# A hybrid retention / attention layer on one core: the opening rebuilt by channel pairs, and transposes woven into three projections

## What is computed

```
mod  = silu(c) @ w_ada + b_ada                    # 6 x 1024; one vector for latents, one for the prompt
h    = rmsnorm(x) * (1 + scale1) + shift1
proj = h @ w_in                                   # q_r,k_r | v_r | g_r | q_d | k_d | v_d | gates
branch_r = (silu(g_r) * group_norm(retention)) @ w_ret_out
branch_d = rmsnorm(diff_attention) @ w_diff_out
x  = x + gate1 * ((gate_r * branch_r + gate_d * branch_d) @ w_o)
h2 = rmsnorm(x) * (1 + scale2) + shift2
x  = x + gate2 * ((silu(h2 @ w_gate) * (h2 @ w_up)) @ w_down);  y = rmsnorm(x)
```

## Time and profile before

| | |
|---|---|
| the profiled execution's own time | 1375.61 us |
| its span (first to last instruction) | 1373.9 us |
| PE busy, PEld busy | 1307.0 us (95%), 1199.1 us (87%) |
| DVE, ACT, POOL busy | 635.4 (46%), 420.0 (31%), 179.8 (13%) |
| share of PE in the chain that ended last | 83% |
| mean granted TensorE clock | 0.986 |

### The profile page before, as it was taken

The page is one execution under the profiler, slowest core; times in us unless marked ns, Lnnn a source line. Parts: engine busy times, 40 slices in busy tenths (PEclk is TensorE's granted clock), DMA queues, the critical chain, the costliest instruction groups (busy, mean ns, idle before and its releaser), DMA issues.

```text
span 1373.9 us, 20027 instructions
## 1 busy us (share of the span) xinstructions
PE 1307.0 (95%) x7974; PEld 1199.1 (87%) x7974; DVE 635.4 (46%) x1001; ACT 420.0 (31%) x642; POOL 179.8 (13%) x189
## 2 busy tenths in 40 slices
PE   4899999999999999998999799899999999999996
PEld 1599887799999999987788798799998999889995
DVE  3734121466657634372898554452224232343245
ACT  5422233344321122213777222242221121212222
POOL 1002000310001011111899200000000000000000
PEclk9999999999999999998999999999999999999998
DMA  9534222143334443452000215111222122221211
GB/s 299 160 103 121 90 64 75 38 154 122 115 130 143 130 121 97 125 188 85 2 2 1 93 62 184 62 62 61 84 69 92 62 69 84 72 82 62 76 46 77
DMA packets 87180, 129.27 MB, mean 94 GB/s; under 512 B 3465, under 2 KB 64386, under 8 KB 86994
## 3 DMA queue, kind: packets, MB, share of 16 engines
q1 hardware_dynamic: 76800, 95.20, 21.3%
q0 software_dynamic: 9104, 32.20, 7.5%
q10 hardware_dynamic: 1218, 1.07, 0.2%
HBM read 117.43 MB, written 4.73 MB: 89 GB/s over the span
## 4 chain that ended last, share of the span: by engine, by line
PE 83%; POOL 6%; DVE 5%; ACT 2%; DMA 2%; issue 1%; DVEq 0%; SPq 0%; ACTq 0%
PE psum L382 50%; PE psum L411 26%; POOL probs L733 3%; POOL probs L739 2%; PE psum L363 1%; DVE ada_acc L1234 1%; DMA x_nat<-in_x_prompt 1%; PE psum L481 1%; PE psum L482 1%; DMA x<-in_x_prompt 1%; PE psum L835 1%; PE psum L833 0%; PE psum L834 0%; DVE hf L524 0%; ACT junk L969 0%
## 5 line engine op out<-in xcount | busy, mean ns | idle before, releaser
L347 DVE TENSOR_TENSOR w_lo<-w_raw,w_hi 128x2048 fp32r<-128x2048 f32 x78 | 178.7, 2291 | 341.5 <-ACT w_hi L342 333.5
L382 PE MATMUL psum<-h_hi,w_lo 128*128 128x320 f32 x1344 | 307.9, 310 | 4.0 <-DVE hf L524 1.4
L382 PE MATMUL psum<-h_lo,w_hi 128*128 128x320 f32 x1344 | 306.8, 309 | 0.0
L382 PE MATMUL psum<-h_hi,w_hi 128*128 128x320 f32 x1344 | 306.8, 309 | 0.0
L382 PEld LDWEIGHTS psum<-h_hi,w_lo 128*128 128x128 f32 x1344 | 225.0, 188 | 5.4 <-issue 4.4
L382 PEld LDWEIGHTS psum<-h_hi,w_hi 128*128 128x128 f32 x1344 | 225.3, 188 | 0.0
L382 PEld LDWEIGHTS psum<-h_lo,w_hi 128*128 128x128 f32 x1344 | 225.1, 188 | 0.0
L342 ACT ACTIVATE w_hi<-w_raw 128x2048 fp32r<-128x2048 f32 x77 | 146.9, 1908 | 209.8 <-PE psum L411 158.5
L411 PE MATMUL psum<-w_lo,h_hi 128*128 128x512 f32 x240 | 93.7, 390 | 0.4 <-ACT mod L1042 0.4
L411 PE MATMUL psum<-w_hi,h_hi 128*128 128x512 f32 x240 | 93.4, 389 | 0.0
L411 PE MATMUL psum<-w_hi,h_lo 128*128 128x512 f32 x240 | 93.4, 389 | 0.0
(11 more groups left out here) (234 smaller groups left out, 1836.3 us busy)
## 6 DMA issues: line engine op xcount, KB each, us to landing
w_raw<-in_w_in SPq DMA_DIRECT2D x32, 1024.0 KB, 5.7
ada_b<-in_w_ada POOLq DMA_DIRECT2D x32, 512.0 KB, 4.0
w_raw<-in_w_ffn_gate SPq DMA_DIRECT2D x11, 1024.0 KB, 5.2
w_raw<-in_w_ffn_up SPq DMA_DIRECT2D x11, 1024.0 KB, 5.2
ada_a<-in_w_ada SPq DMA_DIRECT2D x8, 1024.0 KB, 12.1
w_raw<-in_w_ffn_down SPq DMA_DIRECT2D x8, 1024.0 KB, 4.8
w_raw<-in_w_ret_out SPq DMA_DIRECT2D x4, 1024.0 KB, 4.7
swapped<-qk_d POOLq DMA_DIRECT2D x32, 128.0 KB, 2.5
```

The lines of the kernel that those rows point to most:

```text
L347: dve.tensor_tensor(w_lo[s][:, :, :], w_raw[s][:, :, :], w_hi[s][:, :, :].bitcast(F32), ALU.subtract).then_inc(w_lo_done, 1)
L382: last = pe.matmul(bank(4 * par + 2 * j + h, HALF), w[:, k, cs], x[:, k, h * HALF:(h + 1) * HALF], start=(k == 0 and n == 0), stop=(k == K ...
```

## The change

- SP loads x first, tile by tile, then the first weight tile of w_in, then the tiles of w_ada in pairs: tile n of shift1 and tile n of scale1, which hold the channels of blocks 2n and 2n + 1. The tables and POOL's rope table come later; ACT loads all small rows.
- Six of the eight tiles are now computed directly as columns: `ada_columns` has 128x128 pieces of w_ada as weights and the 2 columns of silu(c) as moving data (16 matmuls a tile). The other two go through DVE as before.
- The transposes of x come early and are copied to SBUF (`x_T`). DVE and ACT modulate pair by pair (`modulate_pair`).
- The first projection works block by block: for each k three of the four halves of units 0 and 1, between them the later `ada_columns`; the fourth half follows at the end. DVE's rotation, split and `setup` of qk_r change order.
- At yg, od and h2 `pe_T_and_dense` issues three blocks of transposes, and then one further block behind each block of products (k + 3 behind k). `dve_to_T_shifted`, `act_to_T_shifted` and DVE's loop for od are as they were.
- ret_out comes ahead of gate_d, right behind the transposes of yg.

```diff
-          ("gate_r", 4, "act", "act"), ("gate_d", 4, "act", "act"), ("ret_out", 4, "dve", "dve"),
+          ("gate_r", 4, "act", "act"), ("ret_out", 4, "dve", "dve"), ("gate_d", 4, "act", "act"),
...
+        x_T = at("x_T", H + 20, [P, KT, TOK])
...
+        def pe_T_and_dense(pe, which, src, name, hi, lo, diagonals=None, by_block=None):
...
+            for k in range(3):
+                block(k)
+            pe_wait_unit(pe, name, 0, 0)
+            for j in range(2):
+                for k in range(KT):
+                    if j == 0:
+                        pe.wait_ge(q["lo"], k + 1)
+                    last = T_products(pe, 0, j, k, hi, lo)
+                    if j == 0 and k + 3 < KT:
+                        block(k + 3)
+                if name in ADA_FIRST and j == 1:
+                    last = pe_ada_sums(pe, name, 0, 0)
+                last.then_inc(mm_done, 1)
+            pe_wait_unit(pe, name, 0, 1)
+            pe_T_unit(pe, name, 0, 1, hi, lo)
+            pe_dense(pe, name, pe_T_unit, hi, lo, first=1)
...
+            pair = 2 + 2 * (k % 3)
+            return psum[:, pair * BANK:pair * BANK + TOK]
...
+            load_first_ada(0, 0, 0)
+            load_first_ada(1, 0, 1)
+            sp.dma_start(w_raw[1][:, :, :], w_in[:, :, UC:2 * UC]).then_inc(w_landed[1], 16)
+            load_first_ada(0, 1, 2)
+            load_first_ada(1, 1, 3)
+            load_first_ada(1, 2, 5)
+            load_first_ada(0, 2, 4)
+            sp.wait_ge(ada_read, 2)
+            load_first_ada(1, 3, 1)
+            load_first_ada(0, 3, 0)
...
+            pool.wait_ge(ada_pre, 16)
...
+            def ada_columns(buf, use, out):
+
+                pe.wait_ge(ada_a_in[buf], 16 * use)
+                for m in range(2):
+                    for k in range(KT):
+                        last = pe.matmul(out[:, 2 * m:2 * m + 2], ada_a[buf][:, k, m * P:(m + 1) * P], silu_c[:, k, :],
+                                         start=(k == 0), stop=(k == KT - 1))
+                return last
...
+            ada_columns(0, 1, shift_and_scale(0, 0)).then_inc(ada_read, 1)
...
+            last = ada_columns(1, 1, shift_and_scale(0, 1))
+            last.then_inc(ada_read, 1)
+            ada_columns(2, 1, shift_and_scale(1, 0)).then_inc(ada_cols, 1)
+            pe.wait_ge(xt_even, 4)
+            pe.wait_ge(xt_odd, 4)
+            three = ((0, 0), (0, 1), (1, 0))
+            for k in range(KT):
+                pe.wait_ge(q["lo"], k + 1)
+                first_products(k, three)
+                if k == 1:
+                    ada_columns(3, 1, shift_and_scale(1, 1)).then_inc(ada_cols, 1)
+                    pe.wait_ge(q["scale"], 1)
+                    ada_columns(4, 1, shift_and_scale(2, 0))
+                    pe.wait_ge(ada_pre, 16)
+                    sums_over_partitions(pe, 0, shift_and_scale(2, 1), ada_acc0).then_inc(ada_cols, 1)
+                if k == 3:
+                    pe.wait_ge(q["scale"], 2)
+                    ada_columns(0, 2, shift_and_scale(3, 0))
...
+            pe.wait_ge(q["scale"], 4)
+            for k in range(KT):
+                first_products(k, ((1, 1),))
+            pe_dense(pe, "qk_r", pe_T_unit, h_hi, h_lo, first=1)
...
-            pe_to_T(pe, "yg", y_nat)
+            pe_T_and_dense(pe, "yg", y_nat, "ret_out", yg_hi, yg_lo)
...
+            pe_T_and_dense(pe, "od", o_nat, "diff_out", od_hi, od_lo, by_block=(norm["normo"]["scaled"], od_scaled))
...
-            pe_to_T(pe, "h2", x1, diag_r)
...
+                if third == 0:
+                    pe_T_and_dense(pe, "h2", x1, "up0", h2_hi, h2_lo, diag_r)
...
+            def modulate_pair(p):
+
+                q, b, two = n2t["h"], 6 + p % 2, slice(2 * p, 2 * p + 2)
+                if p == 0:
+                    dve.wait_ge(ada_read, 2)
+                else:
+                    dve.wait_ge(ada_cols, p + 1)
...
+            modulate_pair(0)
+            first_ada_partial(0, 5, 1)
+            modulate_pair(1)
+            modulate_pair(2)
+            first_ada_partial(1, 1, 2)
+            modulate_pair(3)
```

More of the change, by code:

```diff
@@ L379, in pe_T_unit @@
                         pe.wait_ge(split[0], split[1] + k + 1)
[L380 to L384, removed]
+                    last = T_products(pe, par, j, k, hi, lo)
                 if name in ADA_FIRST and j == 1:
@@ L457, in pe_dense, with tiles_T @@
                     unit(pe, name, i, par, hi, lo, **kw)
-        def pe_to_T(pe, which, src, diagonals=None, by_block=None):
-            q = n2t[which]
[L466 to L475, removed]
+        def tiles_T(pe, which, src, k, pair, diagonals=None):
+            for t in range(TILES):
+                out, x = bank(pair + t // 4, P, (t % 4) * P), src[:, t, k * P:(k + 1) * P]
+                last = pe.matmul(out, x, diagonals[:, t, :], start=True, stop=True) if diagonals is not None else \
+                    pe.transpose(out, x, ident[:, :])
+            last.then_inc(n2t[which]["ps"], 1)
@@ L476, in pe_to_T, with block @@
+        def pe_T_and_dense(pe, which, src, name, hi, lo, diagonals=None, by_block=None):
+            q = n2t[which]
+            def block(k):
                 if by_block is not None:
                     pe.wait_ge(by_block[k % 2], k // 2 + 1)
[L478 to L482, removed]
@@ L705, in _ @@
             pool.wait_ge(r_out, RH * TILES)
-            for name in ("gate_r", "gate_d", "ret_out"):
+            for name in ("gate_r", "ret_out", "gate_d"):
                 with pool.Fori(0, 2) as i:
@@ L787, in _ @@
[L787 to L793, removed]
+            q = n2t["h"]
+            def ada_columns(buf, use, out):
[4 more added lines that the diff above has]
+                                         start=(k == 0), stop=(k == KT - 1))
+                return last
@@ new lines, in shift_and_scale, with first_products @@
+            def shift_and_scale(pair, kind):
+                return bank(6 + pair % 2, 4, 4 * kind)
+            def first_products(k, js):
+                for par, j in js:
+                    if k == 0:
+                        pe.wait_ge(w_lo_done, par + 1)
+                    last = T_products(pe, par, j, k, h_hi, h_lo)
+                    if k == KT - 1:
+                        last.then_inc(mm_done, 1)
+            pe.wait_ge(freed["act"], 2)
+            ada_columns(0, 1, shift_and_scale(0, 0)).then_inc(ada_read, 1)
@@ L1017, in dense, with first_dense @@
+            def first_dense(evacuate):
+                for i in range(2):
+                    for par in range(2):
+                        if i or par:
+                            act_split(act, unit_of("qk_r", i, par) + 1, 1 - par)
+                        if (i, par) == (1, 0):
+                            setup()
+                        evacuate(i, par)
             def dense(name, evacuate):
@@ L1422, in _ @@
             dense("ret_out", gated_ret)
+            dense("gate_d", lambda i, par: None)
             ada_partial("v_d", 0, 0)
```

305 lines of the change are left out of this document (175 added, 130 removed).

## The result

The changed kernel takes 1391.59 us (median of 4 runs, 1390.88 to 1392.43) against 1375.18 us before: a ratio of 1.0122, 95% interval 1.0105 to 1.0140, 16.4 us slower. The forecast was 1390 us, 15 us slower. The profiled execution has a span of 1390.5 us, 16.6 more than before, and a mean clock of 0.977 against 0.986.

The account below looks back on a forecast made before the run. PE was taken to carry the chain almost everywhere, so the start of its products counts. Opening +8, yg +1, od -4 and h2 +10 gave +15 us on 1375.61: 1390.6, taken as 1390 us; 8-in-10 range 1371 to 1402.

Parts of the forecast that it names:

- Opening: Up to v_r's first product: 9 us less at full clock, up to +11 with all clock costs; +8 taken.
- full-clock chain of 109.0 us: Opening with PE always at full clock: qk_r's products end at 109.0 us, 9 us less than 118.06.
- the wait for w_lo: Opening, before qk_r's unit 2: w_lo queued on DVE behind the first tiles' rotation, PE waits 2.6 us.
- the clock's terms: Opening at 1.2 GHz: first column product +3.5, transposes +2.5, narrow stretches +8.8, products behind them +5.1, sum +19.9 us.
- yg: yg and ret_out: products start earlier, but the first unit's sums wait for DVE's accumulations; +1 us (0 to +3).
- od: od and diff_out: six or seven of eight blocks of products lie under DVE's work; -4 us (-5 to -2).
- h2: h2 and up0: serial steps of 3.8 us where PE alone needs 2.0; +10 us (+7 to +17).
- Rival 1: Opening: the clock stays high or recovers at once; opening -9, sum -2, 1373 us; chance 0.13.
- Rival 2: Opening: weight loads do not slow at the lower clock; opening -1.5, sum +5.5, 1381 us; chance 0.16.
- Rival 3: h2: its steps fall to the lower clock too, five steps x 1.7 us more, 1397 us; chance 0.10.
- Rivals 4 and 5: 4: h2's loop does not bind, 1380 us, chance 0.05; 5: 1 and 4 together, 1363 us, chance 0.03.

Follow-up runs that it names:

- the kernel with both repairs: Column products with 128 moving columns and h2's transposes in one piece, against the changed kernel: 1367.15 us, ratio 0.9944 to the kernel before.

## Why the prediction was right

**Opening, +8 forecast, +8.95 measured.** The full-clock chain of 109.0 us is borne out: with 128 columns v_r starts at 112.14 us, of which 2.2 us are the slow first product and 1.6 us the low clock behind the wait for w_lo (29.9 us for 192 products that take 28.4); 108.3 us are left. The wait for w_lo was put at 2.6 us and is 2.7. Of the clock's terms the first product (+3.5) is as forecast. So are the transposes by their size (7.12 against 4.42 us with 128 columns, +2.7; forecast +2.5), but not by their reason: they were put down to the idle start alone, and behind a product of 128 columns they run at the full price. The pair at 34.76 us cost 1.5 and not 3.8 us, as the clock fell later in it than in rows 2 and 3 (PEclk 0.97 from 38 to 40 us, 0.50 from 40 to 43.4); the pair and sums at 50.35 cost 4.2 (forecast 4.7), the single product at 70.06 nothing (forecast 0.3). Behind the three narrow stretches the products cost +1.4, +2.2 and +1.6 (forecast 1.7 each). The step that was missing is the low clock behind the wait for w_lo, +1.6. The terms that the forecast had, 19.9 us by its sum, come to 17 us measured, and to 18.6 with the missing one. The cut from 19.9 to 17 us for an overlap with waits was a guess that the runs don't support: the two waits last 2.7 and 0.5 us with the low clock and 2.6 and 0.5 us with 128 columns, so none of the clock's cost fell under them. That it met the 17 us was luck.

**yg, +1 forecast, +0.1 measured**, within its bounds. The mechanism is the one named, DVE's accumulations end the unit; they ended some 1.6 us earlier than counted (371.54 us, less the shift of 9.15, against 364).

**od, -4 forecast, -3.9 measured**, shown by undoing it (3.8).

**h2, +10 forecast, +11.3 measured.** The forecast's own working gave 10.8 (926.5 - 915.7). First product 6.95 us behind the first transpose by the forecast (897.8 - 890.85), 6.94 measured (903.14 - 896.20); steps 3.8 forecast, 3.89 measured. The PE work of a step was 2.27 us and not 2.0: behind each wait the six products take 1.12 to 1.15 us instead of 0.89, which adds to each step. The reason given (each h_lo stands behind an hf that waits for the next block) is shown by the kernel that changed only the order on DVE and ACT.

**The rivals.** Rival 1 (the clock stays high) is wrong by the windows. Rival 2 (loads don't slow at the lower clock) would make a column product cost 3.5 us at either clock. The measurement decides against it: the eight passes of the first sums, each behind a load of 128 columns, took 1.71 us with PEclk at 0.50 and 0.79 us in the kernel with 128 columns, where PEclk was 1.00; by the pitch it is the same at the start, 6.96 us for 32 passes against 3.47.

```profile
60.80:62.40 1.60, 1.60 (x9) 1.60 (x9) 0.00 (x0) 0.00 (x0) 0.00 (x0) 0.50 0.00 0
```

The Trainium skill, "TensorE: Matmul & The Clock Gate", section "LDWEIGHTS (loading the stationary operand)", gives a load's time as its columns over 1.2 (by estimate 107 ns for 128), and no second value for the lower clock. The 0.11 us a pass at 1.00 agree with it; the 0.21 us at 0.50 do not.

Rival 3 (h2's steps at the lower clock) did not come; its sum should have read 1390 + 8.5 = 1398.5 and not 1397. PE was busy for 15.1 of 25 us there, and PEclk stayed at 1.00:

```profile
900.00:925.00 25.00, 15.09 (x108) 13.98 (x108) 11.54 (x15) 10.48 (x18) 0.00 (x0) 1.00 0.00 1
```

Rivals 4 and 5 turned out to be states that the kernel could be brought into: 4 gave 1380 us for a free loop at h2, and the kernel with h2 in one piece took 1380.77; 5 gave 1363 us for free loops and a high clock, and the kernel with both repairs took 1367.15.

## What to carry to other kernels

Ask of each narrow matmul on the critical path what else could stream for the price of its weight load: padding the moving side to 128 columns cost 0.1 us a column product and gave back 13.6 us. In the opening's 14.9 us, 6.9 are in the narrow matmuls themselves, 5.2 in the broad products behind them and 2.7 in the transposes. Before weaving two stages, walk the consumer's queue: an instruction that waits for the next block must not stand ahead of one that frees this block; and weave only where PE waits within the stage for another engine's blocks (od). At h2 PE had no such wait, and at yg the unit's end hung on DVE's accumulations. A wait for an instruction that stands behind slower work in a queue is handed on to the next such instruction until all of them are moved (one moved: 6 us lost; three: nothing gained; all four, on top of the other repairs: 5.5 us gained).

## What the runs showed of the hardware that was not expected

- At the full clock a pass of a 128x128 weight takes 0.11 us whether 2, 8 or 128 columns of float32 stream (3.47 us for 32 passes with 2 columns and with 8, 7.15 / 2 with 128). Only with 128 did the clock stay up: 8 columns left it at 0.50 in the same window.
- Out of the idle start PE is slow with 128 columns too, but for less time: the first product took 5.75 and 6.50 us in two kernels with 128 columns and the transposes behind it 4.4, against 6.96 and 7.12 with 2 columns and 6.97 and 6.13 with 8. After 4.3 us of matmuls that compute nothing the first product took 3.81 us. PEclk reads 1.00 in all of these; that it was the lower level is worked out from the durations.
- The low stretch at a joint of two phases comes and goes between profiles: gate_r's first unit took 15.72 us in the changed kernel's and 14.18 in that with the idle matmuls, ret_out's second unit 15.72 us with 128 columns and 14.19 with h2 in one piece besides. One such stretch is 1.5 us, more than some of the terms above, so single profiles were read place by place and totals only from medians. What sets it off at a joint stays open.
